# Rotary embedding in a two-block transformer kernel: the quarter turn on VectorE, 32 partitions at a time, in place of a product with a permutation matrix

## What is computed

```python
def rope(x, pos):
    d = x.shape[-1]                       # 64
    ...
    x1, x2 = xf[..., : d // 2], xf[..., d // 2:]
    rot = jnp.concatenate([-x2, x1], axis=-1)
    return (xf * cos + rot * sin).astype(x.dtype)

aq = rope(rms_norm(aq.reshape(B, S, ATTN_HEADS, HEAD_DIM), q_norm_w[l]), pos)
ak = rope(rms_norm(ak.reshape(B, S, ATTN_KV_HEADS, HEAD_DIM), k_norm_w[l]), pos)
...
rq = rope(rq.reshape(B, S, RET_HEADS, HEAD_DIM), pos)
rk = rope(rk.reshape(B, S, RET_HEADS, HEAD_DIM), pos) * (HEAD_DIM ** -0.5)
```

## Time and profile before

| | |
|---|---|
| median of 3 runs | 2057.59 us (2056.57 to 2058.78) |
| the profiled execution | 2056.5 us, its span 2054.7 us |
| TensorE busy | 2017.2 us, 98% |
| VectorE busy | 857.2 us, 42% |
| ScalarE busy | 768.9 us, 37% |
| GpSimd busy | 742.8 us, 36% |
| granted TensorE clock, mean | 0.999 |

### The profile page before, as it was taken

The page is one execution under the profiler, slowest core; times in us unless marked ns, Lnnn a source line. Parts: engine busy times, 40 slices in busy tenths (PEclk is TensorE's granted clock), DMA queues, the critical chain, the costliest instruction groups (busy, mean ns, idle before and its releaser), DMA issues. The chain is left out here.

```text
span 2054.7 us, 27445 instructions
## 1 busy us (share of the span) xinstructions
PE 2017.2 (98%) x9476; PEld 1589.2 (77%) x9476; DVE 857.2 (42%) x1248; ACT 768.9 (37%) x1170; POOL 742.8 (36%) x295
## 2 busy tenths in 40 slices
PE   7999999999999999999989999999999999999999
PEld 5777778888888788888767776767788887888887
DVE  4677674332324443342385555444311264222200
ACT  5344342232223323222255555655522343222211
POOL 2221324444442344443322232222344433444443
PEclk9999999999999999999999999999999999999999
DMA  4211236553322555542212221111123322333322
GB/s 150 62 42 52 62 113 203 185 173 93 110 87 89 183 185 193 194 166 98 83 52 72 61 72 52 51 57 55 62 92 94 100 84 91 95 98 94 113 85 96
DMA packets 56641, 210.72 MB, mean 103 GB/s; under 512 B 6288, under 2 KB 7056, under 8 KB 56592
## 3 DMA queue, kind: packets, MB, share of 16 engines
q1 hardware_dynamic: 56592, 210.08, 31.7%
HBM read 207.96 MB, written 2.10 MB: 102 GB/s over the span
## 5 line engine op out<-in xcount | busy, mean ns | idle before, releaser
L368 POOL TENSOR_TENSOR wlo<-raw,whi 128x1024 fp32r<-128x1024 f32 (+1 forms) x290 | 739.5, 2550 | 1274.0 <-ACT whi L855 1274.0
L413 PE MATMUL bank<-xh,whi 128*128 128x512 f32 x1688 | 681.7, 404 | 19.4 <-DVE xl L1367 12.9
L413 PE MATMUL bank<-xh,wlo 128*128 128x512 f32 x1688 | 660.2, 391 | 0.0
L413 PE MATMUL bank<-xl,whi 128*128 128x512 f32 x1688 | 659.7, 391 | 0.0
L855 ACT ACTIVATE whi<-raw 128x1024 fp32r<-128x1024 f32 (+1 forms) x298 | 330.2, 1108 | 627.1 <-PE bank L413 614.0
L413 PEld LDWEIGHTS bank<-xh,whi 128*128 128x128 f32 x1688 | 317.9, 188 | 97.7 <-issue 22.1
L413 PEld LDWEIGHTS bank<-xl,whi 128*128 128x128 f32 x1688 | 318.4, 189 | 69.4 <-issue 7.7
L413 PEld LDWEIGHTS bank<-xh,wlo 128*128 128x128 f32 x1688 | 317.9, 188 | 67.3
L413 PE MATMUL bank<-acth,whi 128*128 128x512 f32 x528 | 209.3, 396 | 0.5 <-POOL wlo L368 0.5
L413 PE MATMUL bank<-acth,wlo 128*128 128x512 f32 x528 | 209.1, 396 | 0.0
L413 PE MATMUL bank<-actl,whi 128*128 128x512 f32 x528 | 209.1, 396 | 0.0
(11 more groups left out here) (311 smaller groups left out, 2013.7 us busy)
## 6 DMA issues: line engine op xcount, KB each, us to landing
raw<-w_dram SPq DMA_DIRECT2D x250, 512.0 KB, 3.6
adaw<-ada_dram SPq DMA_DIRECT2D x72, 512.0 KB, 4.3
raw<-wd_dram SPq DMA_DIRECT2D x48, 704.0 KB, 4.1
h<-x_dram SPq DMA_DIRECT2D x4, 512.0 KB, 7.4
out_dram<-h SPq DMA_DIRECT2D x8, 256.0 KB, 3.7
rel<-rel_dram SPq DMA_DIRECT2D x1, 513.0 KB, 7.8
crow<-c_dram SPq DMA_DIRECT2D x1, 512.0 KB, 3.4
gates_raw<-gates_dram SPq DMA_DIRECT2D x1, 384.0 KB, 8.3
```

The source lines that it names most:

```text
L368: nc.gpsimd.tensor_tensor(wlo[:, s, 0:width], raw[:, s, 0:width], whi[:, s, 0:width].bitcast(F32), ALU.subtract).then_inc(sem("w_lo"), 1)
L413: mm = nc.tensor.matmul(proj[b][:], w[:, s, W], v[:, k, :], start=first and j == 0 and a == 0, stop=last and j == len(chunks) - 1 and a == ...
```

## The change

The turn is no longer made on TensorE. VectorE multiplies 32 partitions of `rraw` by the same partitions of `sin` and writes the result to the neighbouring 32 partitions of `rt` (`rope_turned`); four such instructions turn a tile. The sign is in the table of sines. `rot` and its transfer go. The order in a mixing step changes too: the queries' rotation stands before the last maxima, the keys' quarters stand in pairs around a scaling, and `ret_queries` stands behind the decays, before the scans.

```diff
--- before.py
+++ after.py
@@ -139,7 +139,6 @@
         lgp = sb("lgp", [P, RH], F32, abs_)
         cos = sb("cos", [P, S], F32, abs_)
         sin = sb("sin", [P, S], F32, abs_)
-        rot = sb("rot", [P, P], F32, abs_)
         leconst = sb("leconst", [P, P], F32, abs_)
         rraw = sb("rraw", [P, 2, S], F32, abs_)
         rsq = sb("rsq", [P, S], F32, abs_)
@@ -309,8 +308,8 @@
             load_wide(None, 2, 0, 1)
             load_x(2)
             load_x(3)
-            for dst, at, n in ((blk, P, P), (rot, 2 * P, P), (sin, 5 * P + S, S), (cos, 5 * P, S), (ident, 0, P), (ge, 3 * P, P),
-                               (leconst, 4 * P, P)):
+            for dst, at, n in ((blk, P, P), (sin, 4 * P + S, S), (cos, 4 * P, S), (ident, 0, P), (ge, 2 * P, P),
+                               (leconst, 3 * P, P)):
                 sp.dma_start(dst[:], const_in[:, at:at + n]).then_inc(sem("const_in"), 16)
             sp.dma_start(rel[:], rel_in).then_inc(sem("rel_in"), 16)
             sp.dma_start(gates_raw[:], gates_in).then_inc(sem("gates_in"), 16)
@@ -472,12 +471,11 @@
             pe.wait_ge(sem("ones"), 1)
 
 
-            def sums_and_turn(p):
+            def rope_sums(p):
 
                 pe.wait_ge(sem("rope_raw"), p + 1)
                 pe.wait_ge(sem("rope_out"), primed(p))
                 nc.tensor.matmul(bank[5][:], blk[:], rsq[:], start=True, stop=True).then_inc(sem("rope_ss"), 1)
-                nc.tensor.matmul(bank[6][:], rot[:], rraw[:, p % 2, :], start=True, stop=True).then_inc(sem("rope_rot"), 1)
 
             def win_scores(t, b):
 
@@ -528,15 +526,6 @@
                                               start=j == 0, stop=j == hi - lo, skip_group_check=True)
                 mm.then_inc(sem("values"), 2)
 
-            def ret_turn(t, j):
-
-                pe.wait_ge(sem(f"evac{j}"), primed(t * 2 + (TILE["ret"] // 2 + 1)))
-                if j == 0:
-                    pe.wait_ge(sem("rope_out"), primed(t * 2 + QT))
-                else:
-                    pe.wait_ge(sem("rope_part"), t * 4 + (2 * QT + 1))
-                nc.tensor.matmul(bank[4][:], rot[:], rraw[:, j, :], start=True, stop=True).then_inc(sem("rope_rot"), 1)
-
             def ret_keys_turn(t):
 
                 pe.wait_ge(sem("rope_out"), primed(t * 2 + (QT + 2)))
@@ -599,9 +588,7 @@
                     if b + 1 < NB:
                         win_scores(t, b + 1)
                     if b == 1:
-                        wide("ret", t, 4, 1, part=(0, 3))
-                        ret_turn(t, 0)
-                        wide("ret", t, 4, 1, part=(3, 6))
+                        wide("ret", t, 4, 1, part=(0, 6))
                     elif b == 0:
                         if t > 0:
                             wide("ret", t, 4, 0, part=(0, 4))
@@ -610,8 +597,6 @@
                     else:
                         for j, lo, hi in RET_BESIDE[b]:
                             wide("ret", t, 4, j, part=(lo, hi))
-                    if b == 2:
-                        ret_turn(t, 1)
                     win_values(t, b)
                 ret_keys_turn(t)
                 ret_scores()
@@ -635,7 +620,7 @@
                 wide("att", 0, 2, p, part=(0, KC // 2))
                 if p == 1:
                     pe.wait_ge(sem("const_ready"), 1)
-                sums_and_turn(p - 1)
+                rope_sums(p - 1)
                 if p == N_ATT - 1:
                     win_scores(0, 0)
                 wide("att", 0, 2, p, part=(KC // 2, KC))
@@ -1432,37 +1417,43 @@
                 V.tensor_tensor(pT[:, p % 2, :] if p < QT else vraw[:], proj[p % 2][:], rstd[:], ALU.mult).then_inc(sem(f"evac{p % 2}"), 1)
 
             att_scaled(0)
-            dve.wait_ge(sem("const_in"), 16 * 7)
+            dve.wait_ge(sem("const_in"), 16 * 6)
             V.tensor_copy(identb[:], ident[:])
             V.tensor_copy(geb[:], ge[:])
             V.tensor_copy(leb[:], leconst[:]).then_inc(sem("const_ready"), 1)
 
 
-            def rope_part(p, slot, turned, part):
-
-                if part == 0:
-                    dve.wait_ge(sem("rope_rot"), p + 1)
+            def rope_turned(p, slot, quarters):
+
+                if quarters[0] == 0:
                     dve.wait_ge(sem("rope_out"), primed(p))
-                    V.tensor_tensor(rt[:, 0, :], bank[turned][:], sin[:], ALU.mult).then_inc(sem("rope_part"), 1)
-                else:
-                    V.tensor_tensor(rt[:, 1, :], rraw[:, slot, :], cos[:], ALU.mult).then_inc(sem("rope_part"), 1)
+                for q in quarters:
+                    R, O = slice(q * 32, q * 32 + 32), slice((q ^ 1) * 32, (q ^ 1) * 32 + 32)
+                    V.tensor_tensor(rt[O, 0, :], rraw[R, slot, :], sin[R, :], ALU.mult).then_inc(sem("rope_part"), 1)
+
+            def rope_straight(slot):
+
+                V.tensor_tensor(rt[:, 1, :], rraw[:, slot, :], cos[:], ALU.mult).then_inc(sem("rope_part"), 1)
 
             def normed_rope(p, dst):
-                for part in range(2):
-                    rope_part(p, p % 2, 6, part)
-                dve.wait_ge(sem("rope_part"), p * 2 + 2)
+                dve.wait_ge(sem("rope_raw"), p + 1)
+                rope_turned(p, p % 2, range(4))
+                rope_straight(p % 2)
+                dve.wait_ge(sem("rope_part"), p * 5 + 5)
                 V.tensor_tensor(rt[:, 0, :], rt[:, 0, :], rt[:, 1, :], ALU.add).then_inc(sem("rope_sum"), 1)
                 dve.wait_ge(sem("rope_sum"), p + 1)
                 dve.wait_ge(sem("rope_rstd"), p + 1)
                 V.tensor_tensor(dst, rt[:, 0, :], rr[:], ALU.mult).then_inc(sem("rope_out"), 1)
 
-            def ret_rope(t, j, part):
+            def ret_rope(t, j, quarters=(), rest=False):
 
                 p = t * 2 + (QT + j)
-                if part < 2:
-                    rope_part(p, j, 4, part)
-                else:
-                    dve.wait_ge(sem("rope_part"), p * 2 + 2)
+                if quarters:
+                    dve.wait_ge(sem(f"evac{j}"), primed(t * 2 + (TILE["ret"] // 2 + 1)))
+                    rope_turned(p, j, quarters)
+                if rest:
+                    rope_straight(j)
+                    dve.wait_ge(sem("rope_part"), p * 5 + 5)
                     V.tensor_tensor((rqf, rkf)[j][:], rt[:, 0, :], rt[:, 1, :], ALU.add).then_inc(sem("rope_out"), 1)
 
             def ret_tile(t, j):
@@ -1565,7 +1556,11 @@
                 for b in range(NB):
                     if b > 0:
                         win_scale(t, 2 * b)
+                        if b == 3:
+                            ret_rope(t, 1, (2, 3))
                         win_scale(t, 2 * b + 1)
+                    if b == 2:
+                        ret_rope(t, 0, range(4), rest=True)
                     if b == 1:
                         if tail:
                             ret_gated(t - 1)
@@ -1578,12 +1573,9 @@
                     if b == 1 and tail:
                         ret_out(t - 1)
                     if b == 2:
-                        for part in range(3):
-                            ret_rope(t, 0, part)
                         ret_tile(t, 1)
-                ret_queries(t)
-                for part in range(3):
-                    ret_rope(t, 1, part)
+                        ret_rope(t, 1, (0, 1))
+                ret_rope(t, 1, rest=True)
                 ret_tile(t, 2)
                 ret_keys(t)
                 dve.wait_ge(sem("decay"), t + 1)
@@ -1591,6 +1583,7 @@
                     ret_decayed(t, e)
                 dve.wait_ge(sem("y_hi"), t + 1)
                 V.tensor_tensor(chunk(yl, t * 2), bank[7][:], chunk(yh, t * 2).bitcast(F32), ALU.subtract).then_inc(sem("y_lo"), 1)
+                ret_queries(t)
                 ret_scans(t)
                 if more:
                     win_maxima(t + 1, 0)
@@ -1984,17 +1977,12 @@
     ident = np.eye(P, dtype=np.float32)
     blk = (p[:, None] // DH == p[None, :] // DH).astype(np.float32)
 
-    rot = np.zeros((P, P), np.float32)
-    for o in range(P):
-        if o % DH < DH // 2:
-            rot[o + DH // 2, o] = -1.0
-        else:
-            rot[o - DH // 2, o] = 1.0
     ge = np.where(p[None, :] >= p[:, None], 0.0, NEG).astype(np.float32)
     le = np.where(p[None, :] <= p[:, None], 0.0, NEG).astype(np.float32)
     inv = (np.float32(10000.0) ** (-np.arange(0, DH, 2, dtype=np.float32) / np.float32(DH))).astype(np.float32)
     ang = inv[p % (DH // 2)][:, None] * np.arange(S, dtype=np.float32)[None, :]
-    const = np.concatenate([ident, blk, rot, ge, le, np.cos(ang), np.sin(ang)], 1).astype(np.float32)
+    sign = np.where(p % DH < DH // 2, 1.0, -1.0)[:, None]
+    const = np.concatenate([ident, blk, ge, le, np.cos(ang), sign * np.sin(ang)], 1).astype(np.float32)
     diff = p[None, :] - p[:, None]
     every = np.ones((P, 1))
     resets = np.ones((P, S // NB, NB))
```

## The result

| | before | changed |
|---|---|---|
| median of the paired runs, us | 2058.04 (2056.57 to 2058.78) | 2088.89 (2087.46 to 2089.92) |
| profiled execution, us | 2056.5 | 2087.46 |
| its span, us | 2054.7 | 2085.7 |
| granted clock over the span | 0.999 | 0.991 |

The ratio is 1.0152, 95% interval 1.014 to 1.0164: slower by 30.9 us where 22.5 were forecast, and 0.9 us above the upper end of the range. The side was right, the size was not.

What follows compares the result with a forecast made beforehand. TensorE is busy 98%, but the attention tiles' loop through VectorE and ScalarE is as long and each mixing step's end waits on VectorE. 7.4 + 2.2 + 10.3 + 2.6 = 22.5 us slower, forecast 2080 us, range 2065 to 2088.

Steps and rivals of the forecast that it cites:

- +3.43 for each of steps 2 to 4: Mixing steps 2 to 4: last scaling ends 3.79 us later, less TensorE's 0.36 wait for keys; +10.3 us in all.
- +2.6 for step 1: Mixing step 1: rotation fits VectorE's 5.19 us idle, but GpSimd's request delays the maxima by 1.25 us; +2.6 us.
- Quarters of 0.68, spaced 0.72, held by the change of partitions: VectorE's turn: each quarter waits for the last one's end, 2.88 us for four; without holding, 5.7 us less overall.
- A GpSimd request in a run costs 2.20: Port shared with GpSimd: a GpSimd request falling into a run of VectorE ops with SBUF inputs costs it 2.20 us.
- Attention period 9.13: Attention tiles: VectorE's loop of 6.93 plus the GpSimd block, against 7.29; four periods at +1.84, +7.4 us.
- Tail up to `win_scale(0,1)`, +2.2: Fifth attention tile: scores 0.90 earlier, quarters add 2.27, block 2.20 where the scaling lost 1.34; TensorE waits for `win_scale(0, 1)`.
- The scaling of tile 6 held for 1.85: Mixing steps 2 to 4: GpSimd takes the port, so the scaling due at 131.1 ends at 132.9, 1.85 us more.
- TensorE idle over 3 us, no wait for the keys: Mixing steps: TensorE idles over 3 us before each step's last transposes; its 0.36 us wait for rotated keys goes.
- The order is hidden, the moved query products cost nothing: Mixing steps: moved query products (2.30 us) fall into the 3.78 us VectorE idles before the scans, at no cost.
- The 11.7 us of the turn are not gained: Thirteen removed TensorE products, 0.90 us each, 11.7 us in all, gained only where TensorE comes last.
- the rival without GpSimd: Rival: quarters don't quarrel with GpSimd; attention period 6.93, +3.5 us together, 2061 us; chance 0.09.

Runs made afterwards that it cites:

- The idle products: Changed kernel plus unread TensorE products in its waits (8 and 4 per mixing step, 12 before `vraw`'s transposes): 2079.9 us, ratio 1.0117.
- one group of partitions: Changed kernel with all four quarters reading and writing partitions 0 to 31 only: 2080.28 us, ratio 1.011.
- the order alone: Kernel before, turn still on TensorE, with VectorE's mixing-step instructions in the order of the change: 2057.27 us, ratio 1.000.
- The kernel with early scalings: Changed kernel with rraw in PSUM, `vraw` evacuated earlier, and the scalings of tiles 6 and 7 moved ahead of GpSimd's product: 2050.16 us, ratio 0.9964.
- rraw in PSUM: Changed kernel with the tile to be turned kept in a PSUM bank instead of SBUF: 2073.79 us, ratio 1.009.
- the short GpSimd product: Changed kernel with GpSimd forming only 8 of 1024 columns of each low part in the first 22 slabs: 2049.44 us, ratio 0.9969.
- the two with the change in one place only: Quarters only in the attention tiles (edit of the kernel before), 2068.21 us; quarters only in the mixing steps (edit of the changed kernel), 2078.03 us.
- once the scalings stood first: Kernel with rraw in PSUM, keys' quarters moved behind both scalings, queries' straight part and sum behind the maxima: 2059.77 us, ratio 1.0009.

## Why the prediction was wrong

The mechanism was right and the sum was one term short: **the step that failed is the costing of the mixing steps, +3.43 for each of steps 2 to 4 and +2.6 for step 1, in which TensorE's new waits were counted at their own length and nothing for the granted clock that falls behind them.** Measured were +5.12, +5.07, +5.01 and +6.0, together 8.3 us more than forecast; the rest of the difference (-0.6 in the attention periods, -0.7 ahead of them, +1.4 near 1240 us) nearly cancels. The prediction had read the clock as 1.00 in the earlier trace rows and carried it over to a kernel that waits over 3 us where the old one never did. The idle products restore the clock and leave the waits' cause in place; there step 1 costs +2.4 and two of the other three +3.2 and +3.05, and `kT` of step 4 comes 22.5 us later than before, the predicted sum (that the sums meet so closely is luck: one fall of the clock that remained, +1.4, is made up for by periods and steps a little shorter than forecast). The Trainium skill ("TensorE: Matmul & The Clock Gate", Why this matters for your kernels) warns of such gaps in TensorE's work; here the stretches of the waits of 3.21 and 1.33 us show 0.67 and 0.64, and shorter waits cost the clock too (last section).

Point by point:

- *Quarters of 0.68, spaced 0.72, held by the change of partitions*: right. 0.683 median, four in 2.82; on one group of partitions four take 2.48. What that is worth in the whole was forecast at 5.7 us and was 8.6 by the medians, but 2.6 between the two profiled executions. That the shorter waits leave the clock up more often would fit, but wasn't tried apart.
- *A GpSimd request in a run costs 2.20*: right, 2.11 (4.93 against 2.82), and it goes when rraw is in PSUM or GpSimd is brief. The Trainium skill ("SBUF — State Buffer", SBUF: two separate sides) has it that GpSimd and VectorE lock one port pair for a whole instruction, for VectorE where both inputs are in SBUF; the trace agrees, with one quarter of 2.80 in a blocked group. The scaling reads only one tensor, in SBUF, and was held as well (2.12 for 0.35).
- *Attention period 9.13*: 9.02; four periods +6.8 for +7.4.
- *Tail up to `win_scale(0,1)`, +2.2*: +2.2. The block fell on the straight product (2.75 at 69.81) and the scaling was free, otherwise than the earlier trace rows suggested. The wait itself was misread: what TensorE waits for at the end of the attention tiles is `vraw` (3.74 us), and `win_scale(0,1)`, done 0.46 us after it, costs nothing more.
- *The scaling of tile 6 held for 1.85, TensorE idle over 3 us, no wait for the keys*: right: 1.77 (2.12 less 0.35), 3.21 and 1.33, and none.
- *The order is hidden, the moved query products cost nothing*: right, by the run with the order alone.
- *The 11.7 us of the turn are not gained*: right for the change. The kernel with early scalings gains 6.8 of them.
- *Rivals*: the period of 6.9 that the rival without GpSimd named is what rraw in PSUM and the short GpSimd product give (6.90, 6.92). Its period would have been right for those kernels; its time of 2061 was not met by either (2073.8 and 2049.4), and for this kernel the period is 9.02.

Open: why one idle-product step still lost its clock, why the same wait costs the clock in one execution and not in another, and whether the change would beat the kernel before with GpSimd out of the way.

## What to carry over

A new wait on TensorE, where it was never idle, can have two prices, its length and the slower clock behind it; here the second was 2 us on top of 3 in each of steps 2 to 4. Before moving work to VectorE, look which of its operands are in SBUF while GpSimd runs, and put short work that TensorE waits for ahead of GpSimd's start and ahead of the long moved piece. Taking off TensorE 11.7 us of products paid only once the operand was in PSUM and the order had been changed as well; either alone was still slower than before.

## What the runs showed of the hardware

- Twelve useless products in each step's waits, 0.26 to 0.3 us each, and twelve ahead of `vraw`'s transposes made the kernel faster, by 7 to 9 us in all.
- The clock did not fall behind every wait. One of 1.50 us in each of steps 2 to 4 left it at 1.00; 3.21 and 1.33 behind each other took it to 0.67 and 0.64 in two stretches of 5 us. In the attention tiles two waits of 2.3 us passed without a trace and behind the third it fell to 0.70.
- The length of the wait alone doesn't decide it. The wait of 2.00 us near 1240 us is the same in all fourteen kernels; the clock fell behind it in three of the profiled executions (the change, and the two with the change in one place only) and stayed at 1.00 in the other eleven. A wait of 2.83 us for `vraw` left it at 1.00 with rraw in PSUM and took it to 0.68 and 0.64 once the scalings stood first. Waits of 1.38 and 1.39 us for `qall`'s product took it to 0.56 in one kernel and left it at 1.00 in the next. A fall near 1240 us costs about 1.4 us, so two profiled executions can differ by that much without a reason in the change.
